# Loading the projection weights first, constants from a second queue, and projecting the first tile block by block

## The reference, cut to what matters

```python
def project(h, pos, w_in):               # h = rms_norm(x, g_pre_mix)
    z = h @ w_in                         # (T, 1024) @ (1024, 1816)
    q = rope(z[..., :512]); kv_c = z[..., 512:768]
    kv_s = rope_kv(z[..., 768:1024]); kv_w = rope_kv(z[..., 1024:1280])
    gates = z[..., 1280:1304]; u = z[..., 1304:]
...
# sample rows: blocks of 32 rows of a paged cache are summed with weights
past_c = cache_kv_cmp[pt]
summ = einsum('nlcgd,lcd->ncgd', blocks(past_c), cmp_pos)
...
x = x + rms_norm(merge(o_cmp, o_sel, o_win, gates, pool_mix(u), w_out), g_post_mix)
x = x + rms_norm((silu(h @ w_gate) * (h @ w_up)) @ w_down, g_post_ffn)
```

## Time and profile before

| | |
|---|---|
| three timed runs | 1767.69 us median (1766.34 to 1768.9) |
| profiled execution | 1768.32 us, of which span 1766.1 us |
| busy share of the span | PE 90%, DVE 45%, ACT 29%, POOL 15% |
| first matmul of the projection | 44.81 us from the span's start |

### The profile page before, as it was taken

One profiled execution on the slowest core, in us unless ns is written; L12 is line 12 of the kernel. 1 busy time (PEld: TensorE's weight loads), 2 busy tenths in 40 slices (PEclk: granted clock), 3 DMA queues, 4 the chain that ended last, 5 costly groups with the idle time before them and its releaser, 6 DMA issues.

```text
span 1766.1 us, 26162 instructions
## 1 busy us (share of the span) xinstructions
PE 1588.8 (90%) x9881; PEld 1049.9 (59%) x9881; DVE 799.1 (45%) x1546; ACT 511.1 (29%) x927; POOL 262.3 (15%) x287
## 2 busy tenths in 40 slices
PE   0998885489999988999799899999999999999994
PEld 0444443467887875776545466666666665666663
DVE  4899975567777783555555311111111111010105
ACT  4222211024444444444333322222222221111105
POOL 0344326300000110000221011111111110000002
PEclk9999997599999999999899899999999999999996
DMA  8666633020000005555220111111111122121102
GB/s 331 228 202 200 177 98 104 0 96 1 1 1 1 1 1 215 212 210 169 90 70 32 48 48 48 48 48 48 48 48 48 48 56 66 33 65 33 33 0 113
DMA packets 96951, 146.29 MB, mean 83 GB/s; under 512 B 7335, under 2 KB 78327, under 8 KB 94639
## 3 DMA queue, kind: packets, MB, share of 16 engines
q1 hardware_dynamic: 85375, 78.45, 14.3%
q0 software_dynamic: 11520, 67.11, 11.0%
HBM read 135.92 MB, written 14.04 MB: 85 GB/s over the span
## 4 chain that ended last, share of the span: by engine, by line
PE 77%; DVE 16%; DMA 2%; issue 2%; ACT 1%; SPq 1%; POOL 0%; DVEq 0%; POOLq 0%; ACTq 0%
PE psum L1496 42%; PE psum L754 6%; PE psum L780 6%; PE psum L1463 5%; DVE arena L1992 4%; PE psum L1096 3%; DVE arena L1991 3%; PE psum L768 3%; PE psum L1037 2%; PE psum L1049 2%; PE psum L2057 2%; PE psum L1075 1%; PE psum L438 1%; DMA arena<-in_cache_kv_sel,sel_idx 1%; DMA arena<-in_cmp_pos 1%
## 5 line engine op out<-in xcount | busy, mean ns | idle before, releaser
L1496 PE MATMUL psum<-arena 128*128 128x384 f16 (+1 forms) x4752 | 734.6, 318 | 5.4 <-POOL arena L1441 2.8
L1496 PEld LDWEIGHTS psum<-arena 128*128 128x128 f16 x4752 | 466.3, 98 | 273.6 <-issue 10.4
L2057 PE MATMUL psum<-arena 128*128 128x512 f16 (+1 forms) x864 | 179.9, 371 | 21.4 <-DVE arena L2036 21.4
L1733 DVE SCALAR_TENSOR_TENSOR arena<-psum,arena 128x384 f32<-128x384 f32 (+1 forms) x66 | 35.3, 536 | 350.1 <-ACT arena L1602 350.1
L2057 PEld LDWEIGHTS psum<-arena 128*128 128x128 f16 x864 | 87.5, 102 | 109.6 <-issue 36.9
L780 PEld LDWEIGHTS psum<-arena 128*128 128x128 f32 x1056 | 136.2, 193 | 11.8 <-issue 6.7
L780 PE MATMUL psum<-arena 128*128 128x64 f32 x1056 | 138.0, 267 | 0.0
L754 PE MATMUL psum<-arena 128*128 128x512 f32 (+3 forms) x384 | 129.7, 461 | 1.7 <-DVE arena L600 1.7
L1602 ACT ACTIVATE arena<-psum 128x384 f32<-128x384 f32 (+1 forms) x66 | 31.2, 473 | 338.9 <-PE psum L1496 338.9
L1441 POOL TENSOR_TENSOR arena<-arena 128x384 f32 (+1 forms) x66 | 57.7, 874 | 465.3 <-ACT arena L1604 465.3
L1850 POOL DMA_INDIRECT arena<-in_cache_kv_cmp,cmp_idx x64 | 82.6, 1290 | 159.1 <-DVE arena L1992 102.4
(11 more groups left out here) (247 smaller groups left out, 1682.4 us busy)
## 6 DMA issues: line engine op xcount, KB each, us to landing
arena<-in_w_gate SPq DMA_DIRECT2D x22, 512.0 KB, 4.0
arena<-in_w_up SPq DMA_DIRECT2D x22, 512.0 KB, 5.3
arena<-in_w_down SPq DMA_DIRECT2D x8, 1408.0 KB, 7.1
arena<-in_x_prompt SPq DMA_DIRECT2D x16, 512.0 KB, 4.0
arena<-in_w_in SPq DMA_DIRECT2D x8, 908.0 KB, 18.7
arena<-in_cache_kv_win SPq DMA_DIRECT2D x8, 512.0 KB, 3.4
out_y_prompt<-arena SPq DMA_DIRECT2D x8, 512.0 KB, 2.6
out_kv_win_sample<-in_cache_kv_win SPq DMA_DIRECT2D x1, 4032.0 KB
```

The lines of the kernel that those rows point to most:

```text
L1496: ins = pe.matmul(out[:, 0:c1 - c0], w[wp][:, k, :], x[xp][:, k, c0:c1], start=(k == 0 and i == 0), stop=(k == n_k - 1 and i == 2))
L2057: ins = pe.matmul(dst[:, 0:n], hT[s][xp][:, k, :], w_in[wp][:, k, c0:c0 + n], start=(k == 0 and i == 0), stop=(k == KD - 1 and i == 2))
```

## The change

SP now issues x tile 0, then the w_in blocks; x tile 1 goes between blocks 3 and 4, `cmp_pos` between blocks 6 and 7, the pooling scale and the FFN gain behind block 7. The constants, the page table and the mixing gain are issued by ACT on its own queue, and the mixing gain has a semaphore of its own. POOL's gathers wait in addition for block 5. ACT does one root of a constant before its first sum of squares. The high and low halves of tile 0 are made after block 0 has been split, the statistics and scaling of tile 1 between blocks 3 and 4. PE projects tile 0 block by block into all four results at once (`project_first`), and its tiles 0 to 7 are written out instead of looped.

```diff
@@ sync
-            sp.dma_start(cst, a["consts"][:, 0:NEARLY]).then_inc(const_loaded, 16)
-            ptab = a["page_table"].rearrange("b j -> j b")
-            for q in range(4):
-                sp.dma_start(pt_i[q::4, :], ptab, ...).then_inc(const_loaded, 16)
             sp.dma_start(x_slot[0], x_prompt[0]).then_inc(x_loaded[0], 16)
-            sp.dma_start(x_slot[1], x_prompt[1]).then_inc(x_loaded[1], 16)
-            sp.dma_start(g_cols[:, 0, :], a["g_pre_mix"]...).then_inc(misc_loaded, 16)
-            sp.dma_start(g_cols[:, 1, :], a["g_pre_ffn"]...).then_inc(misc_loaded, 16)
-            sp.dma_start(scale_cols, a["pool_scale"]...).then_inc(misc_loaded, 16)
-            sp.dma_start(cmp_pos, a["cmp_pos"]...).then_inc(misc_loaded, 16)
             for k in range(KD):
-                if k >= IN_SLOTS:
+                if k == 4:
+                    sp.dma_start(x_slot[1], x_prompt[1]).then_inc(x_loaded[1], 16)
+                if k == IN_SLOTS:
+                    sp.dma_start(cmp_pos, a["cmp_pos"]...).then_inc(misc_loaded, 16)
                     sp.wait_ge(in_split, k - IN_SLOTS + 1)
                 sp.dma_start(raw_in[k % IN_SLOTS], w_in_v[:, k, :]).then_inc(w_in_loaded[k], 16)
+            sp.dma_start(scale_cols, a["pool_scale"]...).then_inc(misc_loaded, 16)
+            sp.dma_start(g_cols[:, 1, :], a["g_pre_ffn"]...).then_inc(misc_loaded, 16)
@@ gpsimd
             pool.wait_ge(idx_ready, 4)
+            pool.wait_ge(w_in_loaded[5], 16)
@@ scalar
+            act.dma_start(cst, a["consts"][:, 0:NEARLY]).then_inc(const_loaded, 16)
+            ptab = a["page_table"].rearrange("b j -> j b")
+            for q in range(4):
+                act.dma_start(pt_i[q::4, :], ptab, ...).then_inc(const_loaded, 16)
+            act.dma_start(g_cols[:, 0, :], a["g_pre_mix"]...).then_inc(gain_loaded, 16)
             act.wait_ge(const_loaded, 80)
+            nc.scalar.activation(x_stat[:, 2:3], const("eps"), ACT.Sqrt).then_inc(act_step, 1)
+            step.at(1)
             stats(0, 0, 16)
-            high(0, 0)
             for k in range(KD):
+                if k == 1:
+                    high(0, 0)
+                if k == 4:
+                    stats(1, 1, 16)
                 act.wait_ge(w_in_loaded[k], 16)
...
-            stats(1, 1, 16)
@@ vector
-            dve.wait_ge(misc_loaded, 64)
+            dve.wait_ge(gain_loaded, 16)
...
             scale(0, 0)
             gain(0, 0)
-            low(0, 0)
             for k in range(KD):
+                if k == 1:
+                    low(0, 0)
+                if k == 4:
+                    scale(1, 1)
                 dve.wait_ge(in_high, k + 1)
...
+            dve.wait_ge(misc_loaded, 48)
@@ tensor
+            def project_first():
+                for k in range(KD):
+                    pe.wait_ge(in_split, k + 1)
+                    for dst, c0, n in ((zq, 0, ATT), (zkw, ATT + 2 * KVR, KVR + NGATE), (zkc, ATT, 2 * KVR), (zu, ATT + ZKV, PW)):
+                        for i, (xp, wp) in enumerate(((0, 0), (0, 1), (1, 0))):
+                            ins = pe.matmul(dst[:, 0:n], hT[0][xp][:, k, :], w_in[wp][:, k, c0:c0 + n],
+                                            start=(k == 0 and i == 0), stop=(k == KD - 1 and i == 2))
+                        if k == KD - 1:
+                            ins.then_inc(z_done, 1)
+                    if k == KD // 2:
+                        turn(1, 1)
...
             turn(0, 0)
-            pe.wait_ge(in_split, KD)
-            with pe.Fori(0, NT // 2) as m:
-                for s in range(2):
-                    tile(m * 2 + s, s, True)
+            for t in range(NT):
+                tile(t, t % 2, True)
             tile(NT, 0, False)
```

More of the change, by code:

```diff
@@ L314, in program @@
         kT_ps = psum[:, 7, :].rearrange("p (k n) -> p k n", n=P)
+        gain_loaded = sem("gain_loaded")
         const_loaded, misc_loaded = sem("const_loaded"), sem("misc_loaded")
@@ L1777, in _ @@
                 sp.sem_inc(free, n)
-            sp.dma_start(cst, a["consts"][:, 0:NEARLY]).then_inc(const_loaded, 16)
-            ptab = a["page_table"].rearrange("b j -> j b")
-            for q in range(4):
-                sp.dma_start(pt_i[q::4, :], ptab, allow_slow_non_contiguous=True).then_inc(const_loaded, 16)
             sp.dma_start(x_slot[0], x_prompt[0]).then_inc(x_loaded[0], 16)
-            sp.dma_start(x_slot[1], x_prompt[1]).then_inc(x_loaded[1], 16)
[L1785 to L1788, removed]
             w_in_v = a["w_in"].rearrange("l (k p) n -> p (l k) n", p=P)
             for k in range(KD):
-                if k >= IN_SLOTS:
+                if k == 4:
+                    sp.dma_start(x_slot[1], x_prompt[1]).then_inc(x_loaded[1], 16)
+                if k == IN_SLOTS:
+                    sp.dma_start(cmp_pos, a["cmp_pos"].rearrange("o l c d -> o (l c) d").broadcast_to([P, 2 * LC, HD])).then_inc(misc_loaded, 16)
                     sp.wait_ge(in_split, k - IN_SLOTS + 1)
                 sp.dma_start(raw_in[k % IN_SLOTS], w_in_v[:, k, :]).then_inc(w_in_loaded[k], 16)
+            sp.dma_start(scale_cols, a["pool_scale"].rearrange("l (k p) -> p (l k)", p=P), allow_slow_non_contiguous=True).then_inc(misc_loaded, 16)
+            sp.dma_start(g_cols[:, 1, :], a["g_pre_ffn"].rearrange("l (k p) -> p (l k)", p=P), allow_slow_non_contiguous=True).then_inc(misc_loaded, 16)
             new_win = a["cache_kv_win"].rearrange("l b w k g d -> (l b) w (k g d)")
@@ L1851, in _ @@
                                              bass.IndirectOffsetOnAxis(ap=cmp_idx[:, k:k + 1], axis=0)).then_inc(cmp_loaded[k % RAW], 16)
-            pool.wait_ge(misc_loaded, 64)
+            pool.wait_ge(misc_loaded, 48)
             for s in range(RAW):
@@ L1861, in _ @@
             step = Chain(act, act_step)
+            act.dma_start(cst, a["consts"][:, 0:NEARLY]).then_inc(const_loaded, 16)
+            ptab = a["page_table"].rearrange("b j -> j b")
+            for q in range(4):
+                act.dma_start(pt_i[q::4, :], ptab, allow_slow_non_contiguous=True).then_inc(const_loaded, 16)
+            act.dma_start(g_cols[:, 0, :], a["g_pre_mix"].rearrange("l (k p) -> p (l k)", p=P), allow_slow_non_contiguous=True).then_inc(gain_loaded, 16)
             act.wait_ge(const_loaded, 80)
+            nc.scalar.activation(x_stat[:, 2:3], const("eps"), ACT.Sqrt).then_inc(act_step, 1)
+            step.at(1)
             def stats(t, s, n):
@@ L2003, in tile @@
                 if more:
-                    scale(t + 1, 1 - s)
+                    if not (isinstance(t, int) and t == 0):
+                        scale(t + 1, 1 - s)
                     gather(t, 0)
@@ L2059, in project @@
                 ins.then_inc(z_done, 1)
+            def project_first():
[9 more added lines that the diff above has]
+                        turn(1, 1)
             def tile(t, s, more):
                 pe.wait_ge(hT_ready, t + 1)
[L2064 to L2069, removed]
+                if t == 0:
+                    project_first()
+                else:
+                    project(zq, s, 0, ATT)
+                    project(zkw, s, ATT + 2 * KVR, KVR + NGATE)
+                    if more:
+                        turn(t + 1, 1 - s)
+                    project(zkc, s, ATT, 2 * KVR)
+                    project(zu, s, ATT + ZKV, PW)
                 pe.wait_ge(q_roped, t + 1)
```

## The result

Four runs of the changed kernel gave 1777.35 us (1775.58 to 1778.72) beside 1767.68 of the kernel before: a ratio of 1.0054, 95% interval 1.0038 to 1.007. It is slower by 9.7 us. The forecast was 1776, slower with a chance of 0.50.

A forecast was written before the change was run, and what follows sets the result against it. DVE was taken to set the pace from the first gathered chunk to the ninth tile; its first rotation moving from 53.5 to 62 us adds 8.5 to the profiled 1768.3, giving 1776.8, by the median 1776.2; range 1757 to 1782.

The forecast's parts named there:

- page table used: ACT's queue at the start: 68 turns beside SP's long rows, 17 us from about 4.5, so constants complete near 22.
- gain landed: Mixing gain behind the table in ACT's queue: 65 pieces beside block 6, cmp_pos and the gathers, landing near 33 us.
- scale, turn, gain: Preparing x tile 0 once the gain is in: 4.3 us as before, ending at 37.3.
- PE's first block: Start of PE's tile 0 projection, after split 0 (2.06 us) and low (1.25): 40.6 us.
- first rotation: DVE's first rotation, after PE's tile 0 (22.1 us) and q's copy: at 62 us instead of 53.5.
- shift there: Delay of DVE's first rotation, +8.5 us, carried unchanged through to the kernel's whole time.
- the price of a four-byte piece: In ACT's queue, each small piece costs one turn of a w_in row, 0.275 us; chance 0.53.
- two bounds: Price of small pieces in ACT's queue: from below 2.8 us of landing as before, from above 68 turns.
- PE's slow start: PE's tile 0: the first 24 matmuls took 7.92 us instead of 5.3, adding 2.7; without it, +6.5 us in all.
- the two signs of being wrong: In the changed kernel's profile: the table lands within 5 us, or the rotation's shift isn't the span's.
- Rival 1: Small pieces in ACT's queue go in groups or slip in between: rotation at 40.6, 1760 us; chance 0.33.
- The Trainium skill's rule: DMA queues take turns by packets of some 9 to 17 descriptors; the table would need 4 to 8 turns.

The follow-up runs named there:

- half_rows: The changed kernel with each w_in block loaded in two halves, rows of 3632 bytes instead of 7264: 1765.01 us, ratio 0.9976 to the kernel before.
- w_in_held: The changed kernel with SP waiting for the constants, page table and mixing gain before it issues w_in: 1766.13 us, ratio 0.9983 to the kernel before.
- small_sp_copy_late: As small_loads_on_sp, with the two DRAM copies issued behind the token stores, near 300 us: 1758.44 us, ratio 0.9947 to the kernel before.
- small_loads_on_sp: The changed kernel with page table and mixing gain issued first of all in SP's queue, constants left with ACT: 1765.04 us, ratio 0.9981 to the kernel before.
- gain_on_sp: The changed kernel with only the mixing gain issued first on SP, the page table left in ACT's queue: 1766.75 us, ratio 0.999 to the kernel before.

## Why the prediction was right

| step | forecast | measured |
|---|---|---|
| page table used | near 22 us | 18.12 |
| gain landed | near 33 | 34.5 |
| scale, turn, gain | 4.3 us | 4.3 (34.53 to 38.84) |
| PE's first block | 40.6 | 41.98 |
| first rotation | 62 | 63.22 |
| shift there | +8.5 us | +9.8 |
| median | 1776 | 1777.35 |

The term that decided was the price of a four-byte piece, taken from above: one turn of a w_in row. half_rows and w_in_held show this mechanism, and the packet counts show it as one to one. That it holds for four-byte pieces was a choice between two bounds, made at 0.53 from rows of long packets; that the kernel came out slower, at 0.50, is in so far luck.

The table was 4 us early. A turn took 0.24 us where I had 0.275, since x rows and completions are among the turns. ACT issued its first load at 0.76 us, 0.9 before SP its own, and by 5 us some 260 of the four-byte pieces were through (279 packets under 512 B, 16 of them the constants' completions), 16 turns for each engine, before w_in stood beside them. The other 52 at 0.24 us are 12.5, which gives 17.5. (The recorded terms, six and a half blocks at 2.2 and x at 1.2, add up to 15.5 and not to the 17 written there; with 17 the table came out at 22, with 15.5 it would have been 20.)

The gain was 1.5 late: its 65 pieces took 16.4 us behind the table's, where I had 11. The queues' packets from 18 to 24, from 24 to 28.5 and from 28.5 to 34.5 us say beside what:

```profile
q1 hardware_dynamic: 375, 2.51, 102.0%
q10 hardware_dynamic: 374, 0.00, 3.6%
...
q1 hardware_dynamic: 118, 1.84, 96.7%
...
q10 hardware_dynamic: 121, 0.00, 1.5%
...
q0 software_dynamic: 560, 2.04, 86.6%
q10 hardware_dynamic: 459, 0.00, 4.7%
```

First w_in rows, 0.26 us a turn; then mostly the 16 KB rows of `cmp_pos`, 0.6 us a turn; then the gathers' 4 KB packets, 0.16 us a turn at first (199 of each queue from 29 to 31 us). The gathers were counted about rightly: 560 packets are 35 turns where I had 36, in 6 us where I had 5. The rest of the difference is w_in: since the table was through 4 us early, w_in rows that I had put beside the table stood beside the gain. That is why the gain landed near the forecast although both parts were off: what it waits for in the end is the rest of SP's queue in front of it.

The rest held: PE and not DVE ends tile 0 (idle 3.06 us before the rotation), no wait for the fifth chunk, steady tiles unchanged, the pieces written out free. Two small slips did no harm: without PE's slow start the terms give +6.1 and not +6.5, and PE's room per steady tile in the earlier trace rows is 2.1 us (25.60 less 23.54), not over 3. One of the two signs of being wrong needs an answer: the rotation's shift should be the span's. The median's 9.7 us against 9.8 says that it is; the profiled execution alone shows 7.7, and 1.2 of the 2.1 missing went in the ninth tile, whose 18.41 us at a clock of 1.00 stand against 19.57 at 0.94 before.

Rival 1, the path that wins, was priced at 1760 and measures 1765.04 where the small loads are out of the way. Its mechanism, the DRAM copy giving back what is won, was right; three terms were small. Block 7 came at 35.1 and not 33, the pooling scale and FFN gain, which I had counted at nothing, held DVE 1.46 us, and the delayed gather took 17.7 us and not 15.3.

The Trainium skill's rule ("DMA: Bandwidth & Descriptors", Queues, rings and completion order) of some 9 to 17 descriptors in a turn was weighed too narrowly: I let only the small pieces go in groups. If both queues did, the counts over a long stretch would be one to one as well and the time the same. The short stretches above decide it: 8 against 8, 7 against 7 and 9 against 9 in 0.3 us each are single packets in turn, and this trace does not agree with that rule. The Trainium skill's statement in the same page (Issuing engines are not separate DMA queues) that a second issuing engine saves only issue time does not hold for this kernel either: the second queue put small pieces behind long rows, which cost 12.3 us against one queue (1777.35 to 1765.04).

## What to carry to other kernels

Count transfers on a second queue in packets: here each packet waited for one of the other queue's, with rows of 3.6 to 16 KB there, and paid by that row's length (0.13 to 0.6 us). So a load that is fetched number by number belongs in front of the long rows in their queue, or has to land before they start. When loads are moved forward, look which later transfer moves forward with them (here a DRAM copy with 64 KB packets) and who loads beside it. Moving a copy without a reader to an idle stretch cost nothing measurable here, and together with the order of the small loads it turned a loss of 9.7 us into a kernel 10 us faster than before.

## What the runs showed of the hardware that was not expected

A gather of 512 KB landed in 4.8 to 5.6 us where the DRAM copy was moved away (small_sp_copy_late, the four issued from 42 to 53 us). Beside the copy it took 15.3 us in the kernel before, 17.7 in small_loads_on_sp, and 25.8 and 26.4 in gain_on_sp, for the two issued at 30.1 and 32.1, which had block 7 and the last small loads beside them too. In gain_on_sp two of the POOL instructions that issue gathers took 2.27 and 2.62 us, where the others of that run took 0.94 to 1.82; in the changed kernel, whose queues were as full, the first four took 0.94 to 1.11. Why was not tried. And ACT's table load stands at 4.75 us, before any wait: the root of a constant that the change puts first saved one of two table loads (1.28 us), which no run needed.
